# A chunked state recurrence on TensorE: where each chunk's output products are issued

## What is computed

```
S = S * w_t + (S a_t) b_t^T + v_t k_t^T        (state, 64 x 64)
y_t = S r_t
y = y(forward) + flip(y(backward))
```

## Time and profile before

| | |
|---|---|
| median of three runs | 2727.54 us |
| the profiled execution | 2725.52 us |
| its span, first to last instruction | 2723.7 us |
| TensorE busy | 2659.0 us (98%) |
| VectorE busy | 1398.4 us (51%) |
| ScalarE busy | 745.2 us (27%) |
| mean granted TensorE clock | 0.995 |
| TensorE's share of the chain that ended last | 95% |

### The profile page before, as it was taken

How to read it: one execution, slowest core, us unless ns; L and a number is a source line. 1 busy time by engine, 2 the same in 40 slices (tenths; PEclk the granted TensorE clock), 3 DMA queues, 4 the chain that set the end, 5 groups by cost and what they waited for, 6 DMA issues and landing times.

```text
span 2723.7 us, 61664 instructions
## 1 busy us (share of the span) xinstructions
PE 2659.0 (98%) x27175; PEld 1710.8 (63%) x27175; DVE 1398.4 (51%) x2723; ACT 745.2 (27%) x1566; POOL 214.9 (8%) x184
## 2 busy tenths in 40 slices
PE   7999999999999999999999999999999999999999
PEld 3455555556454545748888544666666677787887
DVE  2677676674222223337778211777877643314541
ACT  3244333442222222111111002443444322311110
POOL 1000000000000002214444000000000000000000
PEclk9999999999999999999999999999999999999999
DMA  7211111111343432344543224212222244356554
GB/s 267 61 48 44 51 51 45 51 48 43 116 116 93 116 111 67 95 130 142 155 124 115 72 72 142 75 53 58 59 60 55 55 124 109 106 153 179 151 149 121
DMA packets 500010, 264.55 MB, mean 97 GB/s; under 512 B 42865, under 2 KB 493889, under 8 KB 499233
## 3 DMA queue, kind: packets, MB, share of 16 engines
q1 hardware_dynamic: 498016, 251.58, 31.9%
q0 software_dynamic: 1728, 9.03, 0.9%
HBM read 255.33 MB, written 5.24 MB: 96 GB/s over the span
## 4 chain that ended last, share of the span: by engine, by line
PE 95%; DVE 2%; DMA 1%; ACT 1%; issue 1%; SPq 0%; DVEq 0%; ACTq 0%
PE psum L515 36%; PE psum L517 15%; PE psum L1190 12%; PE psum L1302 8%; PE psum L549 2%; PE psum L785 2%; PE psum L1019 1%; PE psum L895 1%; PE psum L1007 1%; PE psum L590 1%; PE psum L997 1%; PE psum L758 1%; PE psum L771 1%; PE psum L873 1%; PE psum L731 1%; PE psum L909 1%
## 5 line engine op out<-in xcount | busy, mean ns | idle before, releaser
L515 PE MATMUL psum<-hT,strips 128*128 128x256 f32 (+1 forms) x2234 | 695.0, 462 | 2.4 <-DMA strips<-in_w_in_dram 1.8
L515 PEld LDWEIGHTS psum<-hT,strips 128*128 128x128 f32 x2234 | 414.5, 190 | 228.2 <-issue 192.5
L517 PE MATMUL psum<-hT,strips 128*64 128x512 f32 (+1 forms) x1932 | 403.5, 537 | 4.4 <-DVE arena L2551 2.4
L1302 PE MATMUL psum<-arena,strips 128*128 128x512 f32 (+1 forms) x704 | 227.6, 486 | 0.6 <-DVE arena L2834 0.6
L517 PEld LDWEIGHTS psum<-hT,strips 128*64 128x64 f32 x1932 | 120.9, 137 | 119.4 <-issue 97.6
L1302 PEld LDWEIGHTS psum<-arena,strips 128*128 128x128 f32 x704 | 133.7, 190 | 93.0 <-issue 83.2
L515 PE MATMUL psum<-arena,strips 128*128 128x256 f32 (+1 forms) x416 | 125.9, 461 | 0.9 <-DVE done L2683 0.9
L2834 DVE SCALAR_TENSOR_TENSOR arena<-psum,mod,arena 128x256 f32<-128x256 f32 x24 | 10.9, 481 | 193.7 <-PE psum L1302 193.7
L515 PEld LDWEIGHTS psum<-arena,strips 128*128 128x128 f32 x416 | 78.9, 190 | 45.0 <-issue 36.8
L2216 DVE TENSOR_SCALAR arena<-arena 128x512 f32<-128x512 f32 (+1 forms) x88 | 69.0, 784 | 71.5 <-ACT arena L2068 69.4
L1846 ACT ACTIVATE arena<-psum,arena 128x512 f32<-128x512 f32 (+1 forms) x96 | 58.2, 615 | 151.3 <-DVE arena L2588 151.3
(11 more groups left out here) (306 smaller groups left out, 4110.8 us busy)
## 6 DMA issues: line engine op xcount, KB each, us to landing
strips<-in_w_in_dram SPq DMA_DIRECT2D x152, 512.0 KB, 3.9
strips<-in_ada_w_dram SPq DMA_DIRECT2D x80, 512.0 KB, 4.0
strips<-in_ffn_up_dram SPq DMA_DIRECT2D x46, 512.0 KB, 3.8
strips<-in_ffn_down_dram SPq DMA_DIRECT2D x32, 512.0 KB, 3.9
conv_branch<-in_ffn_up_dram SPq DMA_DIRECT2D x28, 512.0 KB, 4.9
arena<-in_ada_w_dram SPq DMA_DIRECT2D x4, 2048.0 KB, 13.0
strips<-in_w_in_dram SPq DMA_DIRECT2D x32, 256.0 KB, 3.5
strips<-in_a_out_w_dram SPq DMA_DIRECT2D x16, 512.0 KB, 4.5
```

Source lines behind the costliest of these rows:

```text
L515: return pe.matmul(o, lhs, rhs, start=start, stop=stop, skip_group_check=True)
L517: ins = pe.matmul(o[64 * h:64 * h + 64], lhs[:, 64 * h:64 * h + 64], rhs, start=start, stop=stop, skip_group_check=True)
L1302: ins = mm(s.o[:, lo:T], strip[:, b, j, :], hid[:, k, lo:T], k == 0, k == FT - 1)
```

## The change

`outputs_of_states` becomes `outputs_of_state(c, i)`, which issues the four products of one chunk and stands directly behind `state_in(c, i)` (and behind the inverse of a later pair of chunks, where c is 1 or 2). `outputs_of_values` becomes `outputs_of_values(c, i)` and stands directly behind `state_out(c, i)`; chunk 7, which has no `state_out`, keeps its place at the end of the iteration with its wait and its signal. The output bank is taken when the first of them is issued. Operands, number and shape of all products stay; no transfer is touched.

```diff
+                fresh = [True, True]
+
+                def output_bank(i):
+
+                    if ("y", l, i) not in slots:
+                        take(A, "y", l, i)
+                        fresh[:] = [True, True]
+                    return slots["y", l, i].o
+
+                def outputs_of_state(c, i):
+
+                    for d in range(2) if c >= max(c0, 1) else ():
+                        t, back = place(c, d)
+                        for h in range(2):
+                            pe.matmul(output_bank(i)[rows(h), t], GG[rows(h), c, d, :], AR[i % 2][d][rows(h), c, 1, back],
+                                      start=fresh[h], stop=False, skip_group_check=True)
+                            fresh[h] = False
+
+                def outputs_of_values(c, i):
+
+                    if c == NCH - 1:
+                        pe.wait_ge(*slots[f"in{c}", l, i].freed)
+                    for d in range(2) if c >= c0 else ():
+                        t, back = place(c, d)
+                        for h in range(2):
+                            ins = pe.matmul(output_bank(i)[rows(h), t], RV[:, c, d, h, :],
+                                            EE[:, 1, c // 4, d, h, c % 4, back], start=fresh[h], stop=True,
+                                            skip_group_check=True)
+                            fresh[h] = False
+                    if c == NCH - 1:
+                        ins.then_inc(slots["y", l, i].full[0], 1)
...
                         state_in(c, i)
                         if c in (1, 2):
                             through_inverse(i, ahead, c + 1)
-                        if c == NCH - 1:
-                            outputs_of_states(i)
-                            if ahead:
-                                diagonal_blocks(i + 1)
+                        outputs_of_state(c, i)
+                        if c == NCH - 1 and ahead:
+                            diagonal_blocks(i + 1)
                         if c > 0:
                             fill(steps, hop)
                         if c < NCH - 1:
                             state_out(c, i)
+                            outputs_of_values(c, i)
                             fill(steps, hop)
                     fill(steps, everything)
-                    outputs_of_values(i)
+                    outputs_of_values(NCH - 1, i)
                     halved[0] = False
```

## The result

The changed kernel takes **2739.27 us**, the median of four runs (2738.04 to 2741.31). Four runs of the kernel before on the same chip have a median of 2726.36 us, and the ratio is 1.0055 with an interval of 1.0042 to 1.0068. So it is slower by 13 us between the two medians and by about 15 by the ratio. The forecast was 2730, and 2739.27 lies 1.3 us above the upper end of its range.

What follows compares the result with a forecast made beforehand. It took TensorE, busy 98% of the span, as the bound. Terms 6.2 + 2.4 - 1.9 - 0.2 - 3.0 - 1.0 + 0.4 = +2.9 us gave 2728.4 on the profiled execution, 2730 on the median's footing; range 2724 to 2738.

Steps and rivals of the forecast that it cites:

- Part 1: Moved output groups in the chain: same TensorE time in their new place, no second exit; 0 us, bounds -2 to +7.
- Part 2: Moved outputs fill TensorE waits: -1.9 us before layer 1's `state_in(6)`, -0.2 us in layer 0's last iteration.
- Part 3: Shorter stretch from `state_in(7)` to L803 makes TensorE wait for VectorE's list: +6.2 us layer 0, +2.4 us layer 1.
- Part 4: Issue gaps swallowed by the L803 wait: -3.0 us at L749 and L937, -1.0 us at L782 behind it.
- B: Rival, slower: L803 wait at full size in all 14 transitions, no gap swallowed; +9.2 us, 2736.7; chance 0.22.
- C: Rival, faster: dense runs of small instructions broken up, issue gaps vanish throughout the mixing; -6.0 us, 2721.5; chance 0.10.
- the wait at L803 in 14 of 14: Sign at L803: wait by VectorE, about 0.9 us layer 0, 0.3 to 0.7 layer 1, in ten or more of 14.
- L2444 2.48 us behind `state_in(7)`: Sign on VectorE: its list (L2437 before the edit) starts 2.5 us after `state_in(7)`, no longer waiting for L749.
- the hop longer by 0.23: Sign in the chain: each hop becomes 0.23 us longer with each moved group.
- L749's gaps cost nothing: Sign between `state_in(7)` and L803: issue gaps at L749 no longer add time.

Runs made afterwards that it cites:

- late_base: Kernel before, with VectorE's transpose L2496 done twice more in layer 0 and once more in layer 1, TensorE's order untouched; 2734.99 us, ratio 1.0042.
- rebudget: Changed kernel with dense work in each hop that has outputs cut by those outputs' time and put behind the chain; 2738.17 us, ratio 1.0042.
- rebudget_late_diag2: As rebudget, plus a little dense work between the outputs behind `state_in(7)` and `diagonal_blocks(i+1)`; 2726.09 us, ratio 1.0002.
- v5_only2: Kernel before with only layer 1's chunk 5 value outputs moved into the chain, behind `state_out(5)`; 2729.07 us, ratio 1.0014.
- states_only: Changed kernel with the value outputs back in one batch at the iteration's end, only state outputs in the chain; 2727.14 us, ratio 1.0013.

## Why the prediction was wrong

- **Part 1 was right.** In their new place the groups cost 0.23 to 0.24 us (L941) and 0.33 (L930 behind `state_in`, the exit from it included). There is no second exit. The way from the first `state_out` to `state_in(7)` grew by 3.01 us in layer 0, where 3.03 was worked out.
- **Part 2 was right.** The 2.3 us of L895 are gone.
- **Part 3 was right** in its mechanism and near in size: 9.3 us of waits, 14 times, against a forecast of 8.6. In layer 0 they are 5.7 us against 6.2: the forecast had 0.88 each, and there are five of 0.74 to 0.84, one of 1.61 and one of 0.23, where L749 has its long gap. In layer 1 they are 3.6 against 2.4 (0.45 to 0.60 each, where 0.35 was forecast with a rest of 0.3 in the range). late_base shows that such a wait by itself costs about 11 us.
- **Part 4 failed**, in both halves, and this is the step that made the forecast wrong. It said that what L749's and L937's gaps cost would no longer be added, since VectorE sets the time there: -3.0. It overlooked that a gap at L749 delays L749 itself, and so the start of VectorE's list, because `turn_blocks` reads L749's result: the iteration with L749's gap of 1.93 us at 256.03 took 19.87 us from `state_in(7)` to L803, against 18.26 and 18.28 in its neighbours, and still waited 0.23 us there. 1.6 of the 1.93 us came on top. By the same comparison 4.6 of the 5.8 us of all five L749 gaps came on top. Part 4 had also counted 3.4 us of gaps between `state_in(7)` and L803 where there were 5.8, since 2.0 us of them stood at L517. Before, 3.1 of the 5.8 stood behind L749, where a wait for VectorE could have hidden them; after, all of them stand in L749. And it said that L782's gaps would shrink by 1.0, since a waiting TensorE has its instructions nearer: they grew by 1.2 in late_base, which has this wait alone, and by 1.8 after the change. No run shows them shrink by the wait.
- **What the sum left out** is that a gap is not a given sum that hides or shows. In the account of the mixing the changed kernel has +3.7 us of gaps and +3.4 us of low clock, where the sum had -4.0 and 0. These 11 us are the miss: 2.9 + 11.1 = 14.0, against 13.3 measured there. Not all of it can be put down to the change. The +3.7 lie outside the stretch of part 4: L782 has 1.8 of them, L827 has 0.3 ahead of anything that the change touches, and the rest are small gaps at L832, L515 and L840. Of the three low-clock stretches one stands behind that gap at L827 and two behind gaps at L782. late_base, with no product moved, has the same two behind L782. The one stretch of the kernel before stood behind the 2.03 us wait of rows 7. The changed kernel still waits 1.80 us there, without a low clock, and late_base 2.04 us, also without. How much of the 7.1 us is the change's and how much is one execution's chance stays open.
- That the place of dense work among the small products changes the gaps, and the time with them, is shown by rebudget and rebudget_late_diag2: between them only the place of some dense pieces differs, and 11 us of time.
- **The rivals.** B, "the wait in full", was nearest (2736.7), and for its own reason: no gap is swallowed, because they move to other places. Its waits were too long (10.9 against 9.3), and the low clock that it named did come, at 1.7 us a stretch instead of 1.3, but behind issue gaps and not behind the new waits. C had the sign of the gaps wrong: the batches were broken up, and the gaps stayed.
- The signs that were named ahead came out so: the wait at L803 in 14 of 14, L2444 2.48 us behind `state_in(7)` where L749 has no gap, the hop longer by 0.23. "L749's gaps cost nothing" was the one that failed.

The Trainium skill's page Runtime: NRT & Kernel Launch, section Instruction fetch mechanics, tells of instructions being fetched in blocks of 256 while the ones before are executed, and calls the cost of crossing from one block to the next mostly hidden. The traces here agree with the 256, as told below. They agree with "mostly hidden" by count, so the prediction read too much into its gaps: in the mixing of the kernel before, TensorE crosses 153 such places and has a gap of more than 0.25 us at 14 of them. The ones that are not hidden cost 10 to 22 us in the mixing.

**What stays open** is the size of each gap. It is not a fixed time for so many instructions. The 256 instructions that end at the gap in question took 2.97 us before, 3.28 in v5_only2, 4.33 in rebudget and 3.33 in rebudget_late_diag2, the gap included. So what came before them counts as well, and no run here measured the supply by itself. Nor is the size the same from one execution to the next. That the gaps are a shortage of instructions is what their place and their answer to dense work point to; the profile has no record that says so.

## What to carry to other kernels

Moving cheap work forward past another engine's hand-over shortens that engine's deadline by the time moved; here two timelines gave the length of the other engine's list to a tenth of a microsecond, and the sum of the waits as 8.6 us where 9.3 came. Where TensorE runs hundreds of small products close together, look at its idle time without a releaser before reordering: dense work put into the run ahead of such gaps took them from 12.3 to 3.2 us here, and a gap ahead of the step that starts the other engine's list is not hidden by the wait at the list's end. A gap or a low clock of one profile is weak evidence, since both vary between executions. Try a reorder with the dense fills placed anew before judging it: here this alone (the smaller hop and the late `diagonal_blocks` together) brought 1.0055 back to 1.0002.

## What the runs showed of the hardware

- In the kernel before and in the changed one, counting TensorE's loads, products and semaphore instructions together, every gap by "issue" of more than 0.25 us in the mixing (14 and 13 of them) stands 193 or 194 instructions past a multiple of 256. With 128 instructions put in front the gaps stand in other iterations, and again at 193 to 195.
- The same gap varies by chance: the one at L827, ahead of anything that the change touches in layer 0, was 1.40 to 1.48 us in four profiles besides that of the kernel before (1.45), 1.75 or 1.76 in three, 1.13 in rebudget, and absent in states_only, with the same instructions of TensorE ahead of it. The three longest and one of those of 1.44 were followed by a low clock, the other four were not.
- The granted clock fell to half for about 3.4 us behind some idle times of TensorE of 1.44 to 3.16 us, and not behind others of up to 2.34 us; it fell for twice as long twice in rebudget and once in pad128. Kernels with more gaps lose more to it: 0 to 3.4 us with 10 to 13 us of gaps in the mixing, 15.4 us with 22.5.
